# Second product of a PEER layer: a 416 column matmul, or two of 208 into the same columns

## The reference, cut to what matters

```python
ue = jnp.take(u, it, axis=0)                                   # expert rows of u
act = jax.nn.gelu(jnp.einsum('nd,ned->ne', xt, ue), approximate=False) * gt
ve = jnp.take(v, it, axis=0)                                   # expert rows of v
return jnp.einsum('ne,ned->nd', act, ve)
...
x = x + g_c * peer_ffn(...)                                    # then a last RMSNorm
```

## Time and profile before

| | us |
|---|---|
| median of 3 runs | 2674.2 |
| lowest and highest run | 2669.99 and 2680.89 |
| span of the profiled execution | 2669.1 |
| of it: first product's stretch (1275 to 1924) | 649 |
| second product's stretch (1924 to 2654) | 730 |
| end (2654 to 2669) | 15 |

### The profile page before, as it was taken

How to read it: one execution, slowest core, us unless ns; L and a number is a source line. 1 busy time by engine, 2 the same in 40 slices (tenths; PEclk the granted TensorE clock), 3 DMA queues, 4 the chain that set the end, 5 groups by cost and what they waited for, 6 DMA issues and landing times.

```text
span 2669.1 us, 56826 instructions
## 1 busy us (share of the span) xinstructions
PE 2543.1 (95%) x23437; PEld 2347.2 (88%) x23437; DVE 1368.0 (51%) x2443; ACT 1083.5 (41%) x1752; POOL 1634.2 (61%) x844
## 2 busy tenths in 40 slices
PE   5899999989979999999999999999989999999997
PEld 3799999657757999999999999999978888888887
DVE  0450355773226455995574010010178777687777
ACT  1333433341213434444433333333445554555555
POOL 0366677012225776888655777777668777777763
PEclk9899999889988999999999999999999999999999
DMA  9987845577864444444555654754589998999884
GB/s 374 394 288 267 277 167 169 181 278 252 256 224 161 159 172 133 166 157 171 181 184 185 239 203 157 252 200 163 192 294 327 316 379 311 318 367 327 310 304 130
DMA packets 213561, 639.92 MB, mean 240 GB/s; under 512 B 16520, under 2 KB 26264, under 8 KB 183832
## 3 DMA queue, kind: packets, MB, share of 16 engines
q1 hardware_dynamic: 176712, 514.54, 55.7%
q0 software_dynamic: 27472, 97.56, 9.9%
q10 hardware_dynamic: 9216, 25.53, 2.4%
HBM read 605.61 MB, written 31.97 MB: 239 GB/s over the span
## 4 chain that ended last, share of the span: by engine, by line
PE 69%; POOL 9%; issue 9%; DMA 7%; DVE 5%; ACT 1%; POOLq 0%; SPq 0%; DVEq 0%; ACTq 0%
PE bank L929 68%; POOL ring_lo L806 8%; DMA kept<-in_peer_v 3%; DMA kept<-in_w_ada 3%; DVE ring_lo L2782 2%; DVE act_hl L2779 1%; DVE staged L2844 1%; ACT hi_peer L1686 0%; PE bank L932 0%; POOL staged L905 0%; DMA staged<-in_w_ada 0%; DVE staged L2366 0%; DMA staged<-late_acts,staged 0%; POOL ring_lo L813 0%; DVE staged L2390 0%
## 5 line engine op out<-in xcount | busy, mean ns | idle before, releaser
L1686 ACT ACTIVATE hi_peer<-kept 128x1024 fp32r<-128x1024 f32 x544 | 559.3, 1054 | 906.6 <-PE bank L929 758.8
L806 POOL TENSOR_TENSOR ring_lo<-kept,hi_peer 128x1024 fp32r<-128x1024 f32 x288 | 718.7, 2519 | 271.4 <-ACT hi_peer L1686 271.4
L929 PE MATMUL bank<-h_hi,ring_lo 128*128 128x288 f32 x2848 | 838.5, 294 | 0.0
L929 PE MATMUL bank<-act_hl,hi_peer 128*128 128x416 f32 x2048 | 625.6, 370 | 13.9 <-DVE staged L2844 6.4
L929 PE MATMUL bank<-h_hi,hi_peer 128*128 128x288 f32 x2048 | 608.6, 297 | 2.8 <-POOL ring_lo L806 2.6
L929 PE MATMUL bank<-h_lo,hi_peer 128*128 128x288 f32 x2048 | 604.2, 295 | 0.0
L929 PEld LDWEIGHTS bank<-h_hi,ring_lo 128*128 128x128 f32 x2848 | 537.3, 189 | 0.0
L929 PE MATMUL bank<-act_hl,ring_lo 128*128 128x208 f32 x2048 | 528.6, 258 | 0.0
L929 PEld LDWEIGHTS bank<-act_hl,hi_peer 128*128 128x128 f32 x2048 | 385.0, 188 | 53.9 <-issue 40.6
L929 PE MATMUL bank<-staged 64*64 64x64 f32 (+13 forms) x6760 | 385.5, 296 | 31.4 <-issue 19.3
L929 PEld LDWEIGHTS bank<-act_hl,ring_lo 128*128 128x128 f32 x2048 | 391.8, 191 | 0.0
(11 more groups left out here) (261 smaller groups left out, 3107.3 us busy)
## 6 DMA issues: line engine op xcount, KB each, us to landing
kept<-in_peer_u SPq DMA_DIRECT2D x128, 1024.0 KB
kept<-in_peer_v SPq DMA_DIRECT2D x128, 1024.0 KB
kept<-in_w_ada SPq DMA_DIRECT2D x64, 1024.0 KB
kept<-in_w_in SPq DMA_DIRECT2D x50, 1024.0 KB
staged<-in_w_ada SPq DMA_DIRECT2D x32, 1024.0 KB
kept<-in_w_adaf SPq DMA_DIRECT2D x32, 1024.0 KB
kept<-in_w_out SPq DMA_DIRECT2D x16, 1024.0 KB
kept<-in_w_q SPq DMA_DIRECT2D x16, 1024.0 KB
```

The source lines that it names most:

```text
L806: pool.tensor_tensor(ring_lo[:, n % RING_SLOTS, cols], ring[n % RING_SLOTS][:, cols], hi_slot(n)[:, cols].bitcast(F32), ALU.subtract).then ...
L929: return pe.matmul(out, lhsT, rhs, start=start, stop=stop)
L1686: return act.activation(out, in_, ACT.Copy)
```

## The change

The 416 column matmul becomes two of 208 columns with the same weights; the second, high weight x low activation, adds to the same 208 columns that the other two use. The columns 208 to 415 of the banks are no longer written. The eviction then reads 208 columns once.

```diff
-                    hi_lo, out = act_hl[:, slot, e, :], ps[4 + dt]
-                    matmul(out[:, 0:2 * VN], w_hi[:, cols], hi_lo, first and e == 0, False)
-                    mm = matmul(out[:, 0:VN], w_lo[:, cols], hi_lo[:, 0:VN], False, last and e == 3)
+                    hi_lo, out = act_hl[:, slot, e, :], ps[4 + dt][:, 0:VN]
+                    matmul(out, w_hi[:, cols], hi_lo[:, 0:VN], first and e == 0, False)
+                    matmul(out, w_hi[:, cols], hi_lo[:, VN:2 * VN], False, False)
+                    mm = matmul(out, w_lo[:, cols], hi_lo[:, 0:VN], False, last and e == 3)
...
-                    for c in range(2):
-                        ins = stt(out=xo[:, kt, 0:VN], in0=ps[4 + dt][:, c * VN:(c + 1) * VN], scalar=mods[:, G_C, kt, 0:1],
-                                  in1=xo[:, kt, 0:VN], op0=ALU.mult, op1=ALU.add)
-                        if c == 0:
-                            link(ins)
-                    ins.then_inc(S("out_taken"), 1)
+                    stt(out=xo[:, kt, 0:VN], in0=ps[4 + dt][:, 0:VN], scalar=mods[:, G_C, kt, 0:1],
+                        in1=xo[:, kt, 0:VN], op0=ALU.mult, op1=ALU.add).then_inc(S("out_taken"), 1)
```

## The result

| | before | changed |
|---|---|---|
| median, us | 2675.25 (4 runs) | 2729.66 (4 runs) |
| lowest and highest run, us | 2669.99 to 2680.89 | 2727.8 to 2731.42 |
| span of the profiled execution, us | 2669.1 | 2726.0 |

The ratio is 1.0198, with a 95% interval of 1.018 to 1.0216: the changed kernel is 54 us slower. The forecast was 2730.4 us. Its terms are compared with the traces further down, since a sum can also be right by luck.

A forecast was written before the change was run, and what follows sets the result against it. TensorE's matmul stream was taken to bound the kernel, most of all in PEER's second product. Slots +68.6, stalls -12 and end -0.45 gave +56.2 us, so 2726.2 lowest and a 2730.4 us median, range 2690 to 2757.

The forecast's parts named there:

- The bound: PEER's second product lasts as long as TensorE's matmul stream, counted by distances between starts, plus 21.4 us of standing.
- The slot: Second product: each of a triple's three matmuls takes a weight load's 0.1115 us, 0.0335 us more per triple, +68.6 us.
- The upper bound: Second product: all the pair's excess is the short slot's, 0.1143 us a slot, a triple of 0.343 us, +86 us.
- the lower: Second product: the distance between loads may be 0.105 us before rounding, a triple of 0.315 us, +28.7 us.
- The reading of the pair: Kernel before, second product: 0.1115 us for the short matmul's load plus 0.1867 us for 416 columns, near the measured 0.301.
- The stalls: Second product: a longer tile gives the ring and other engines time; 12 of TensorE's 21.4 us of standing go.
- The eviction's share: Changes of pass: one addition instead of two ends six TensorE waits 0.46 us earlier each, 2.8 us in all.
- The end: End of the second product: the last bank's two additions stand before a square and the last sum; halving saves 0.45 us.
- The sum: Whole kernel: +68.6 - 12 - 0.45 = +56.2 us, giving a median of 2730.4 us, 2.1% slower.
- A: Rival, chance 0.07: no load floor for fp32r, 208 columns cost 0.100 us, a triple 0.300 us; 2669 us.
- B: Rival, chance 0.06: loads hide wholly behind streaming, slots about 0.095 us, a triple 0.285 us; 2638 us.
- C: Rival, chance 0.09: the second load of the same weights is free or hidden, a triple 0.323 us; 2707 us.

The follow-up runs named there:

- the runs with 104 and 232 columns: Kernel before with 104 or 232 columns in place of 208 in the short matmul of each pair; 2674.56 us and 2675.29 us.
- the split alone: Kernel before with three matmuls of 208 columns, but two sums in each bank and two additions per eviction as before; 2727.19 us.
- the halved eviction alone: Kernel before with its pairs of matmuls, the second addition of each eviction left out; 2673.69 us.
- the triple in the other order: Changed kernel with the triple ordered high x high, low weight x high, high weight x low; 2729.44 us in a single run.

## Why the prediction was right, point by point

**The bound.** TensorE's stream, counted by distances between starts and not by durations, was the right measure: durations would have said 2 x 0.276 + 0.275 us for a triple.

**The slot (+68.6 us forecast, 70.5 measured).** The step that decided was to look for the floor in matmuls with few columns, though they were plain float32 in another part of the kernel. 0.1115 us was taken, 0.1117 found. The upper bound (0.1143) was 2% high and the lower (0.105) 6% low. The reading of the pair was right too, as the runs with 104 and 232 columns show. One size in it was off: the excess over streaming is not 0.0133 us at every count, but 0.008 at 208 columns and 0.011 at 256.

**The stalls (-12 us forecast, 21.4 - 4.5 = 16.9 measured).** The mechanism was right, more time per tile for the ring and the engines behind it, and the size was too small. I had kept some 9 us, mostly at the start of the product, and half of that went too.

**The eviction's share (2.8 us of those 12).** This step failed as a cause: with the split alone nothing was missed, since the longer tile leaves no wait for the eviction that could be shortened. In the kernel before, the halved eviction alone gained nothing that can be told from noise, and whether it is worth 2.8 us there stays open. VectorE's busy time was to fall to 530 us and fell to 543.80. The additions gave 27.8 us of the 30 (128 of 433 ns became 64), but in the changed kernel each split of activations took 1077 ns where it had taken 957, and each subtraction of 384 columns 656 where it had taken 824; why is open.

**The end (-0.45 us forecast, 0 measured).** From the product's last matmul to the end of the span it is 18.2 us in both kernels. The changed kernel's last matmul of the product, the last sum, and the last eviction and square:

```profile
2707.75 0.27 PE L929 MATMUL bank<-act_hl,ring_lo 128*128 128x208 f32 x1
...
2707.86 2.60 PE L929 MATMUL bank<-staged,kept 128*128 128x288 f32 x10
2708.13 0.43 DVE L2844 SCALAR_TENSOR_TENSOR staged<-bank,kept,staged 128x208 f32<-128x208 f32 x1 [0.90 <-PE bank L929]
...
2708.60 0.44 ACT L1684 ACTIVATE staged<-staged 128x288 f32<-128x288 f32 x1 [0.89 <-DVE staged L2844]
```

The same in the kernel before, TensorE alone:

```profile
2650.87 0.26 PE L929 MATMUL bank<-act_hl,ring_lo 128*128 128x208 f32 x1
2650.97 2.60 PE L929 MATMUL bank<-staged,kept 128*128 128x288 f32 x10
```

The sum's ten matmuls take 2.60 us from first to last in both, and begin 0.10 and 0.11 us after the last matmul of the product. They keep TensorE busy all that time in the records, so an earlier eviction beside them shortened nothing. The step that failed is "stand in front of a square and the last sum": it read two rows of VectorE and ScalarE without TensorE's.

**The sum.** The forecast was +56.2 us, and 54.4 us lie between the medians. The parts agree less well than the total. The second product grew by 50.9 us, where the two measured terms give 70.5 - 16.9 = 53.6 us; the 3 us between them are open. The 56.9 us between the two spans hold 6.0 us from the stages before, so their nearness to 56.2 says little. That the forecast of 2730.4 us came within 0.7 us of the median is luck in part: the term of the slots was 1.9 us too low and the relief of the stalls 4.9 us too small, and the median of the kernel before came out 1.05 us above the 2674.2 us that the sum started from. What was not luck is the size of the slot, which decides the sign and most of the amount. Of the rivals, A and B fell with the slot at 0.1117 us and C with the triple in the other order.

## What to carry to other kernels

A matmul costs the larger of its weight load and its own columns, so splitting one for free columns is not free: below a bend between 232 and 256 streaming columns, with 128 weight columns (float32 in parts), every further split adds a full load, even of the same weights. Count weight loads where moving data are short, and find the floor in the same trace, in any burst of matmuls with few columns. And don't price a saving by the length of one wait: here it was worth nothing once the longer tile had given the whole ring slack. To cost it, ask how much slack the ring has after the change.

## What the runs showed that I had not expected

- The granted clock can fall when TensorE streams less, though it is kept busy by loads: to 0.50 for 34 us with 128 columns a slot, and to 0.83 on average over 786 us with 104 columns and weights of 96 (a single run), where 208 columns gave 1.00. Work left out made the kernel slower by 12 us in the first case. What in the stream decides this was not tested.
- The kernel before spreads over 24 us in 13 runs of one comparison (2662.37 to 2686.43), the one with the split alone over 6 us in 4 (2722.1 to 2728.49), and the changed one over 4 us in 4. Stalls may have a part in it, which was not tested, but much of it arises before the second product: in the traces of the kernel before, the changed one and the one with the halved eviction alone, the second product begins at 1923.1, 1929.1 and 1937.1 us, though nothing ahead of it differs. The granted clock of the first 640 us is 0.95, 0.95 and 0.92 there, and the slower executions mostly have the lower mean clock: 0.967 at 2686.43 us and 0.976 at 2668.34 us.
